# The opening of a decoder block: x by column halves, two weight splits on GpSimd, seven fewer unread products

## The chip, the cores and the metric

The kernel runs on one core of a Trainium2 chip. The metric is the time of one execution on the device in microseconds (us); lower is better. TensorE (PE) multiplies, VectorE (DVE), ScalarE (ACT) and GpSimd (POOL) work element by element, and SyncE (SP) issues nearly all DMAs, in one queue.

## What is computed

One decoder block on 256 tokens of 1024 columns, in float32: a root-mean-square norm of `x`, one combined projection for attention, retention and gates, both branches, a second norm, and a mixture of 32 experts. Around the change only this matters:

```
h = x * lax.rsqrt(jnp.mean(x * x, axis=-1, keepdims=True) + EPS) * g_mix
proj = h @ w_in
```

The later parts (attention, retention, experts, final norm) are the same in both kernels.

## The kernel before

The kernel writes out by hand what each engine does, with a list per engine and semaphores between them. Each engine works through its list strictly in order.

*Float32 products in three parts.* A weight chunk lands in `raw(s)`; ACT rounds it to a high part (`high(Q, s, n)`, one copy of 128x768), and DVE subtracts it from the raw values to a low part (`low(Q, s, n)`). A quad Q has four chunks, s = 0 to 3, and each chunk is used in 18 matmuls of 256 columns in the first two quads. The activation `h`, turned so that columns are on partitions, has a high and a low part too: `normed_high(m)` on ACT and `normed_low(m)` on DVE, m = 0 to 3, two blocks of 128 columns each. PE may start on chunk s of quad 0 when `hT_dve` has reached s + 1 (`normed_low(s)` is done) and `lo_ready` has reached s + 1 (`low(0, s)` is done).

*The opening.* SP issues the two halves of the tokens, t = 0 and 1, as one DMA each (512 KB), then the first weights. For each t ACT squares and sums 1024 columns; DVE scales the sum to a mean square; POOL raises it to the power of minus one half; DVE multiplies the identity by it (`spread`); and PE spreads it over all partitions by a product with ones. ACT copies that to `roots`, and `norm_columns(m)` on DVE multiplies the transposed x by gain and `roots`, two instructions for each m. PE has transposed x in between, into PSUM banks 0 to 3. The first quad writes banks 0 and 1, so that both `norm_columns(0)` and `norm_columns(1)` have to be done before it starts.

*Unread products.* `unread(n)` on PE multiplies the identity by itself n times into a bank that nobody reads. PE runs 6 while x is under way, 2 between the two sets of transposes, 8 behind the product that gives the roots, and 10 more once `norm_columns(0)` is done. The profile counts two records for each of them.

*The order of DVE behind the roots* is written out: `norm_columns(0)`, `norm_columns(1)`, `normed_low(0)`, `low(0,1)`, `normed_low(1)`, and so on. `low(0,0)` stands ahead of the wait for `roots`. SP loads the raw chunk s of quad 1 when `lo_ready` has reached s + 1. POOL has, behind the two powers, four selects of 128x256 that build the attention bias, and then nothing for a long time.

*What follows.* PE goes through four pairs of attention heads, retention, gates and output projection on weights that SP streams in, until the second norm at 322 us. While it does so SP fills free room with the first experts. From 362 us on eight teams of four experts go through PE, each with 24 MB of weights.

Of the kernel before, what the change touches and what calls it, by code (L numbers as in the profile page):

```python
# [24 lines left out]
ALU = mybir.AluOpType  # L25
ACT = mybir.ActivationFunctionType
AX_X = mybir.AxisListType.X
F32 = mybir.dt.float32
# [30 lines left out]
def hybrid_block(nc, x, g_mix, w_in, w_attn, w_ret, w_out, g_ffn, w_router, b_router,  # L59
# [42 lines left out]
    with ExitStack() as ctx:  # L102
# [3 lines left out]
        def sem(name):  # L106
            return ctx.enter_context(nc.semaphore(name))
# [148 lines left out]
        begin_f = gatedT[0:1, PASSES:2 * PASSES]  # L256
        res = hn[:, :, :, :].rearrange("p a k q -> p a (k q)")

        s_x = [sem(f"s_x{t}") for t in range(TT)]
        s_gain = sem("s_gain")  # L260
        s_wr = sem("s_wr")
        s_gk = sem("s_gk")
# [84 lines left out]
        def raw(s, n):  # L347
            return ring[:, 0, s * RAW:s * RAW + n]
# [6 lines left out]
        def is_in_place(Q):  # L355
# [3 lines left out]
        slots = [ring[:, s, :] for s in range(6)] + [oRT_slot[:, :], mid[:, :], store[:, :], hT_slot[:, :],  # L359
                                                         spare[:, :]]  # L360

        MERGED = ((0, 1), (1, 2), (2, 4), (4, 6), (6, 8))
        G_AT, U_AT, D_AT = (3, 4, 5, 10), (7, 0, 1, 2), (8, 9, 6)

# [17 lines left out]
        @block.sync  # L382
        def _(sp):
            for t in range(TT):
                sp.dma_start(xs[:, t, :], x_v[:, t, :]).then_inc(s_x[t], 16)

            def load_quad(Q, piece, after_use=False, fill=(None,) * CH):

# [168 lines left out]
        @block.gpsimd  # L557
        def _(pool):
            link, _n = chain(pool, pool_chain, 0)

            link(pool.memset(ident[:, :], 0.0))
            pool.affine_select(out=ident[:, :], in_=ident[:, :], compare_op=ALU.not_equal, fill=1.0, base=0,
                               pattern=[[-1, P]], channel_multiplier=1).then_inc(const_ready, 1)
            pool.memset(half_neg[:, :], -0.5).then_inc(const_ready, 1)

            def inv_root(n):
                for t in range(TT):
                    pool.wait_ge(ms_done, TT * n + t + 1)
# [12 lines left out]
            pool.affine_select(out=before[:, :], in_=before[:, :], compare_op=ALU.is_gt, fill=0.0, base=0,  # L581
                               pattern=[[1, P]], channel_multiplier=-1).then_inc(const_ready, 1)
            pool.memset(ones[:, :], 1.0).then_inc(const_ready, 1)
            pool.iota(slot_ids[:, :], pattern=[[1, ROUNDS * SLOTS]], base=1, channel_multiplier=0,
                      allow_small_or_imprecise_dtypes=True).then_inc(const_ready, 1)
            pool.iota(rev_ids[:, :], pattern=[[-1, NR]], base=NR, channel_multiplier=0,
                      allow_small_or_imprecise_dtypes=True).then_inc(const_ready, 1)
            pool.iota(expert_ids[:, :], pattern=[[1, E]], base=0, channel_multiplier=0,
                      allow_small_or_imprecise_dtypes=True).then_inc(const_ready, 1)
            link(pool.memset(ident_b[:, :], 0.0))  # L590
            pool.affine_select(out=ident_b[:, :], in_=ident_b[:, :], compare_op=ALU.not_equal, fill=1.0, base=0,
                               pattern=[[-1, NP]], channel_multiplier=1).then_inc(const_ready, 1)
            pool.wait_ge(const_ready, 2)
            inv_root(0)

            for g, (window, _dil) in enumerate(GROUPS):
                if g == 0:
                    pool.wait_ge(dist_done, 1)
                else:
                    pool.wait_ge(dil_done, g)  # L600
                ins = pool.affine_select(out=bias_t[:, g, :], in_=dist if g == 0 else bias_t[:, g, :], compare_op=ALU.is_ge,
                                         fill=MASKED, base=P, pattern=[[-1, T]], channel_multiplier=1)
                if window < T:
                    link(ins)
                    ins = pool.affine_select(out=bias_t[:, g, :], in_=bias_t[:, g, :], compare_op=ALU.is_ge, fill=MASKED,
                                             base=window - P, pattern=[[1, T]], channel_multiplier=-1)
                ins.then_inc(bias_done, 1)
            for i in range(TWOS):
                pool.wait_ge(rvar, i + 1)
                pool.tensor_tensor(out=rstdR[:, :], in0=meanvar[:, :, 1], in1=half_neg[:, :],  # L610
                                   op=ALU.pow).then_inc(rrstd, 1)
            inv_root(1)
            inv_root(2)

        @block.scalar
        def _(act):
            act.dma_start(mix_k[:, :], g_mix.rearrange("(p k) -> p k", k=KT)).then_inc(s_mix, 16)

            def high(Q, s, n):

                act.wait_ge(raw_loaded[s], 32 * Q + 32)
                if not isinstance(Q, int) or Q > 0:

                    act.wait_ge(chunk_used, CH * Q + s + 1 - CH)
                high_of = high_part[:, s, 0:n] if is_in_place(Q) else split[:, s, 0, 0:n]
                act.activation(high_of, raw(s, n), ACT.Copy).then_inc(hi_ready, 1)  # L626

            for t in range(TT):
                act.wait_ge(s_x[t], 16)
                if t > 0:  # L630
                    act.wait_ge(sq_done, t)
                act.activation(junk, xs[:, t, :], ACT.Square, accum_out=ss[:, 0, t:t + 1]).then_inc(sq_done, 1)  # L632

            def normed_high(m):
                act.wait_ge(normed_done, 2 * m + 2)
                act.activation(hT[:, 0, 2 * m:2 * m + 2, :], normed[:, 2 * m:2 * m + 2, :], ACT.Copy).then_inc(hT_act, 1)
# [1 line left out]
            high(0, 0, W_A)  # L638
            act.wait_ge(roots_psum, 1)
            act.activation(roots, bank(4, T), ACT.Copy).then_inc(roots_ev, 1)  # L640
            for m in range(CH):
                normed_high(m)
                if m < CH - 1:
                    high(0, m + 1, W_A)

            def attention(i, n_next):
                for s in range(CH):
# [141 lines left out]
        def _(dve):  # L789
# [22 lines left out]
            for g in range(1, NG):  # L812
# [2 lines left out]
                dve.scalar_tensor_tensor(bias_t[:, g, :], resid_f, MASKED, dist, ALU.mult, ALU.add).then_inc(dil_done, 1)  # L815
                dve.wait_ge(dil_done, g)
            for t in range(TT):
                dve.wait_ge(sq_done, t + 1)
                dve.tensor_scalar(ms[:, 0, t:t + 1], ss[:, 0, t:t + 1], 1.0 / D, EPS, ALU.mult, ALU.add).then_inc(ms_done, 1)
                dve.wait_ge(rstd_done, t + 1)  # L820
                dve.tensor_scalar(spread[:, t, :], ident[:, :], rstd[:, 0, t:t + 1], None, ALU.mult).then_inc(spread_done, 1)
            dve.wait_ge(s_mix, 16)
            low(0, 0, W_A)
            dve.wait_ge(roots_ev, 1)

            def norm_columns(m):

                dve.wait_ge(hT_psum, 3 if m < 2 else 4)
                for k in (2 * m, 2 * m + 1):
                    dve.scalar_tensor_tensor(normed[:, k, :], ps[:, k // 2, (k % 2) * T:(k % 2 + 1) * T], mix_k[:, k:k + 1],  # L830
                                             roots, ALU.mult, ALU.mult).then_inc(normed_done, 1)

            def normed_low(m):
                dve.wait_ge(hT_act, m + 1)
                dve.tensor_tensor(hT[:, 1, 2 * m:2 * m + 2, :], normed[:, 2 * m:2 * m + 2, :],
                                  hT[:, 0, 2 * m:2 * m + 2, :].bitcast(F32), ALU.subtract).then_inc(hT_dve, 1)

            norm_columns(0)
            norm_columns(1)
            normed_low(0)  # L840
            low(0, 1, W_A)
            normed_low(1)
            norm_columns(2)
            low(0, 2, W_A)
            normed_low(2)
            norm_columns(3)
            low(0, 3, W_A)
            normed_low(3)
            dve.wait_ge(bias_done, NG)
# [352 lines left out]
        def _(pe):  # L1202
# [13 lines left out]

            def transpose_rows(t):

                pe.wait_ge(s_x[t], 16)
                rows_t = xs[:, t, :].rearrange("q (p k) -> q k p", k=KT)  # L1220
                for k in range(KT):
                    at = (k % 2) * T + t * P
                    ins = pe.transpose(ps[:, k // 2, at:at + P], rows_t[:, k, :], ident[:, :])
                    if k in (3, 7):
                        ins.then_inc(hT_psum, 1)

# [38 lines left out]
                pe.wait_ge(spread_done, t + 1)  # L1265
                ins = mm(ps[:, 4, t * P:(t + 1) * P], all_ones, spread[:, t, :], True, True)
            ins.then_inc(roots_psum, 1)
            unread(8)
            pe.wait_ge(normed_done, 2)
            unread(10)  # L1270

            with pe.Fori(0, PAIRS) as i:
                queries = columns(NG, 0, W_A)
# [315 lines left out]
```

## Time and profile before

| | before |
|---|---|
| median of 3 runs | 764.15 us (764.02 to 764.28) |
| profiled execution | 763.96 us, its span 762.2 us |
| busy, whole span | PE 599.3 us, DVE 241.5 us, ACT 183.2 us, POOL 11.2 us |
| end of the opening, where the first matmul of quad 0 starts | 12.38 us |

The span begins with the first recorded instruction and ends with the last; 1.8 us of the execution's own time lie outside it. The two times at the ends of the 3 runs are 0.03% apart. All starts below are in us from the start of the span.

### The profile page before, as it was taken

How to read it: one execution, taken by the hardware profiler on the slowest of the kernel's cores; microseconds unless marked ns; L12 is line 12 of the kernel's file. 1: busy time of each engine (PE TensorE's matmuls, PEld its weight loads, DVE VectorE, ACT ScalarE, POOL GpSimd, SP SyncE). 2: the span in 40 equal slices, each digit the busy share in tenths (PEclk: the TensorE clock that was granted, in tenths of full speed). 3: DMA queues.
4: the chain of work that ended last, by engine and by line, in shares of the span. 5: the costliest groups of instructions: out<-in, count | busy, mean ns of one | idle time of the engine just before them, and what ended most of it. 6: DMA issues, size and time to landing. Idle time of an engine off the chain costs nothing.

```text
span 762.2 us, 10787 instructions
## 1 busy us (share of the span) xinstructions
PE 599.3 (79%) x4333; PEld 405.0 (53%) x4333; DVE 241.5 (32%) x411; ACT 183.2 (24%) x250; POOL 11.2 (1%) x31
## 2 busy tenths in 40 slices
PE   9999999999999999999748458458458457556655
PEld 8999999989899999843213113113113113113111
DVE  7667485746554456761010010010010010000001
ACT  5455453644425444341000000000000000000002
POOL 3000000000000000000000000000000000000000
PEclk9999999999999999999979679778877977868979
DMA  8956859564637798979999999999999999999995
GB/s 242 280 158 205 253 151 308 182 202 142 198 119 220 223 329 297 389 312 423 432 426 426 426 427 426 430 426 430 430 423 433 426 423 430 429 426 428 429 416 196
DMA packets 84810, 254.84 MB, mean 334 GB/s; under 512 B 8240, under 2 KB 57392, under 8 KB 72880
## 3 DMA queue, kind: packets, MB, share of 16 engines
q1 hardware_dynamic: 82272, 254.30, 86.6%
q10 hardware_dynamic: 2512, 0.18, 0.2%
q8 instruction: 18, 0.29, 0.1%
q14 instruction: 8, 0.07, 0.0%
HBM read 253.41 MB, written 1.05 MB: 334 GB/s over the span
## 4 chain that ended last, share of the span: by engine, by line
PE 52%; DMA 37%; SPq 7%; ACT 1%; DVE 1%; issue 1%; POOL 0%; POOLq 0%; DVEq 0%; ACTq 0%
PE ps L1204 51%; DMA work<-in_w_down 37%; SPq L540 4%; SPq L492 2%; SPq L461 1%; ACT work L662 1%; DMA store<-in_x 0%; PE ps L1300 0%; PE ps L1410 0%; PE ps L1328 0%; POOL rstd L569 0%; DVE hn L1182 0%; ACT work L632 0%; ACT hn L730 0%; PE ps L1525 0%
## 5 line engine op out<-in xcount | busy, mean ns | idle before, releaser
L1204 PE MATMUL ps<-ring,work 128*32 128x512 f32 x768 | 136.5, 693 | 20.5 <-DMA spare<-in_w_gate 20.3
L1204 PE MATMUL ps<-mid,work 128*32 128x512 f32 (+1 forms) x152 | 77.0, 668 | 71.1 <-DMA ring<-in_w_up 71.1
L1204 PE MATMUL ps<-store,work 128*32 128x512 f32 x128 | 68.3, 692 | 55.5 <-DMA work<-in_w_down 54.1
L1204 PE MATMUL ps<-hT,split 128*128 128x256 f32 x768 | 93.6, 284 | 0.0
L1204 PEld LDWEIGHTS ps<-hT,split 128*128 128x128 f32 x768 | 92.6, 192 | 0.8 <-issue 0.7
L799 DVE TENSOR_TENSOR split<-ring,split 128x768 fp32r<-128x768 f32 (+1 forms) x72 | 73.8, 1045 | 54.8 <-ACT split L626 54.8
L1204 PEld LDWEIGHTS ps<-mid,work 128*32 128x32 f32 (+1 forms) x152 | 20.5, 140 | 125.6 <-DMA ring<-in_w_up 77.5
L1120 DVE TENSOR_TENSOR work<-work,ps 128x512 f32<-128x512 f32 x8 | 5.5, 688 | 240.9 <-PE ps L1204 240.9
L626 ACT ACTIVATE split<-ring 128x768 fp32r<-128x768 f32 (+1 forms) x72 | 64.9, 915 | 70.5 <-PE ps L1204 51.3
L1204 PE MATMUL ps<-split,hT 128*128 128x384 f32 (+1 forms) x384 | 80.4, 365 | 0.0
L1204 PEld LDWEIGHTS ps<-split,hT 128*128 128x128 f32 x384 | 68.8, 188 | 7.8
L1204 PEld LDWEIGHTS ps<-store,work 128*32 128x32 f32 x128 | 15.2, 126 | 101.1 <-DMA work<-in_w_down 57.5
L1204 PE MATMUL ps<-hT_slot,work 128*32 128x512 f32 x128 | 68.3, 692 | 0.0
L1204 PE MATMUL ps<-oRT_slot,work 128*32 128x512 f32 x128 | 68.3, 692 | 0.0
L1204 PEld LDWEIGHTS ps<-ring,work 128*32 128x32 f32 x768 | 33.5, 125 | 65.5 <-issue 40.1
L1204 PE MATMUL ps<-spare,work 128*32 128x512 f32 x128 | 65.0, 665 | 0.0
L796 DVE TENSOR_TENSOR low_part<-ring,high_part 128x1024 fp32r<-128x1024 f32 x36 | 44.1, 1224 | 45.7 <-ACT high_part L626 45.7
L626 ACT ACTIVATE high_part<-ring 128x1024 fp32r<-128x1024 f32 x36 | 38.1, 1058 | 52.7 <-DMA ring<-in_w_in 22.5
L1113 DVE TENSOR_TENSOR work<-ps,gain_s 128x512 f32<-128x512 f32 x14 | 9.7, 692 | 124.1 <-PE ps L1204 124.1
L1204 PE MATMUL ps<-hT,high_part 128*128 128x256 f32 x256 | 46.2, 283 | 0.0
L755 ACT ACTIVATE work<-ps 128x512 f32<-128x512 f32 x8 | 4.8, 597 | 151.0 <-PE ps L1525 151.0
L1204 PE MATMUL ps<-d_home,work 128*32 128x512 f32 x64 | 40.4, 791 | 0.0
(203 smaller groups left out, 779.9 us busy)
## 6 DMA issues: line engine op xcount, KB each, us to landing
ring<-in_w_up SPq DMA_DIRECT2D x21, 2048.0 KB, 43.2
ring<-in_w_gate SPq DMA_DIRECT2D x18, 2048.0 KB, 39.5
ring<-in_w_in SPq DMA_DIRECT2D x80, 256.0 KB, 3.1
ring<-in_w_in SPq DMA_DIRECT2D x96, 192.0 KB, 4.2
mid<-in_w_up SPq DMA_DIRECT2D x7, 2048.0 KB, 34.7
store<-in_w_down SPq DMA_DIRECT2D x6, 2048.0 KB, 34.8
hT_slot<-in_w_down SPq DMA_DIRECT2D x6, 2048.0 KB, 39.2
oRT_slot<-in_w_down SPq DMA_DIRECT2D x6, 2048.0 KB, 43.7
```

Of the source, the lines that this page charges most:

```text
L461: sp.dma_start(slots[at[j]], expert(view, p, j)).then_inc(loaded, 16)
L492: sp.dma_start(d3_home[:, :], expert(wd_v, p, 3)[:, 0:2 * D]).then_inc(down_loaded, 16)
L540: sp.dma_start(to, expert(wd_v, q, j)[:, at:at + n_words]).then_inc(loaded, 16)
L626: act.activation(high_of, raw(s, n), ACT.Copy).then_inc(hi_ready, 1)
L662: act.activation(probsT[u], s_cols(u), ACT.Copy).then_inc(apt_act, 1)
L755: act.activation(hidT.rearrange("p f s -> p (f s)"), bank(0), ACT.Copy).then_inc(hidT_ev, 1)
L796: dve.tensor_tensor(low_part[:, s, 0:n], raw(s, n), high_part[:, s, 0:n].bitcast(F32), ALU.subtract).then_inc(lo_ready, 1)
L799: dve.tensor_tensor(split[:, s, 1, 0:n], raw(s, n), split[:, s, 0, 0:n].bitcast(F32), ALU.subtract).then_inc(lo_ready, 1)
L1113: dve.tensor_tensor(xg[:, steps, :], bank(h).rearrange("p (k s) -> p k s", k=4), gain_s[:, steps].unsqueeze(2).to_broadcast([P, 4, P]), AL ...
L1120: dve.tensor_tensor(hid, sg, bank(3), ALU.mult).then_inc(hid_ready, 1)
L1204: return pe.matmul(o, lhsT=l, rhs=r, start=start, stop=stop, skip_group_check=shared)
```

## The change

Six things are changed, all in the opening.

1. x comes in four DMAs of 256 KB (two column halves of each t) in place of two of 512 KB.
2. ACT squares each half by itself (four squares of 128x512 in place of two of 128x1024). DVE scales the first half's sum ahead of time, and a second instruction of one column adds the other half's.
3. The transposed x goes to PSUM banks 2, 3, 5 and 6, and quad 0 no longer writes over it.
4. DVE does `norm_columns(0)` right behind the roots, then `low(0,0)` and `normed_low(0)`, and only then `norm_columns(1)`.
5. The low parts of chunks 1 and 2 of quad 0 are made by POOL. DVE waits for each at a fixed place in its list (`low_of_pool`), and passes the news on in `lo_ready`.
6. The unread products behind the roots are 6 and 5 in place of 8 and 10.

```diff
-                sp.dma_start(xs[:, t, :], x_v[:, t, :]).then_inc(s_x[t], 16)
+                for h in range(2):
+                    cols = slice(h * HALF, (h + 1) * HALF)
+                    sp.dma_start(xs[:, t, cols], x_v[:, t, cols]).then_inc(s_x[t][h], 16)
...
+            for s in (1, 2):
+                pool.wait_ge(hi_ready, s + 1)
+                pool.tensor_tensor(out=split[:, s, 1, 0:W_A], in0=raw(s, W_A), in1=split[:, s, 0, 0:W_A].bitcast(F32),
+                                   op=ALU.subtract).then_inc(lo_pool, 1)
...
             for t in range(TT):
-                act.wait_ge(s_x[t], 16)
-                if t > 0:
-                    act.wait_ge(sq_done, t)
-                act.activation(junk, xs[:, t, :], ACT.Square, accum_out=ss[:, 0, t:t + 1]).then_inc(sq_done, 1)
+                for h, (part, done) in enumerate(((3, sq_begin), (0, sq_done))):
+                    act.wait_ge(s_x[t][h], 16)
+                    if t > 0:
+                        act.wait_ge(done, t)
+                    cols = slice(h * HALF, (h + 1) * HALF)
+                    act.activation(junk[:, cols], xs[:, t, cols], ACT.Square,
+                                   accum_out=ss[:, part, t:t + 1]).then_inc(done, 1)
...
+                dve.wait_ge(sq_begin, t + 1)
+                dve.tensor_scalar(ms[:, 3, t:t + 1], ss[:, 3, t:t + 1], 1.0 / D, EPS, ALU.mult, ALU.add).then_inc(ms_begin, 1)
+                dve.wait_ge(ms_begin, t + 1)
                 dve.wait_ge(sq_done, t + 1)
-                dve.tensor_scalar(ms[:, 0, t:t + 1], ss[:, 0, t:t + 1], 1.0 / D, EPS, ALU.mult, ALU.add).then_inc(ms_done, 1)
+                dve.scalar_tensor_tensor(ms[:, 0, t:t + 1], ss[:, 0, t:t + 1], 1.0 / D, ms[:, 3, t:t + 1],
+                                         ALU.mult, ALU.add).then_inc(ms_done, 1)
...
+            def low_of_pool(s):
+                dve.wait_ge(lo_pool, s)
+                dve.wait_ge(lo_ready, s)
+                dve.sem_inc(lo_ready, 1)
...
-            unread(8)
+            unread(6)
             pe.wait_ge(normed_done, 2)
-            unread(10)
+            unread(5)
```

The order on DVE in the opening, from the combining of the squares' sums to the end of the opening. In these rows `ms` is written by the scaling, `work<-ident,rstd` is `spread`, `split<-ring,split` is `low`, `hn<-ps,mix_k,work` is `norm_columns` and `hT<-hn,hT` is `normed_low`. Before:

```order
L821 TENSOR_SCALAR work<-ident,rstd 128x128
L799 TENSOR_TENSOR split<-ring,split 128x768
L830 SCALAR_TENSOR_TENSOR hn<-ps,mix_k,work 128x256 x4
L835 TENSOR_TENSOR hT<-hn,hT 128x512
L799 TENSOR_TENSOR split<-ring,split 128x768
L835 TENSOR_TENSOR hT<-hn,hT 128x512
L830 SCALAR_TENSOR_TENSOR hn<-ps,mix_k,work 128x256 x2
L799 TENSOR_TENSOR split<-ring,split 128x768
L835 TENSOR_TENSOR hT<-hn,hT 128x512
L830 SCALAR_TENSOR_TENSOR hn<-ps,mix_k,work 128x256 x2
L799 TENSOR_TENSOR split<-ring,split 128x768
L835 TENSOR_TENSOR hT<-hn,hT 128x512
```

Now:

```order
L840 TENSOR_SCALAR work<-ident,rstd 128x128
L848 SCALAR_TENSOR_TENSOR hn<-ps,mix_k,work 128x256 x2
L814 TENSOR_TENSOR split<-ring,split 128x768
L853 TENSOR_TENSOR hT<-hn,hT 128x512
L848 SCALAR_TENSOR_TENSOR hn<-ps,mix_k,work 128x256 x4
L853 TENSOR_TENSOR hT<-hn,hT 128x512
L848 SCALAR_TENSOR_TENSOR hn<-ps,mix_k,work 128x256 x2
L853 TENSOR_TENSOR hT<-hn,hT 128x512
L814 TENSOR_TENSOR split<-ring,split 128x768
L853 TENSOR_TENSOR hT<-hn,hT 128x512
```

Two of the four `low` rows have left DVE, and the one that stood ahead of the first `norm_columns` stands behind it; the waits for POOL stand between the second and third pair of `norm_columns`, and ahead of the third `normed_low`.

The order on ACT, where `work,ss<-store` is a square, `split<-ring` is `high` and `hT<-hn` is `normed_high`. Before:

```order
L632 ACTIVATE work,ss<-store 128x1024 x2
L626 ACTIVATE split<-ring 128x768
L640 ACTIVATE work<-ps 128x256
L636 ACTIVATE hT<-hn 128x512
L626 ACTIVATE split<-ring 128x768
L636 ACTIVATE hT<-hn 128x512
L626 ACTIVATE split<-ring 128x768
L636 ACTIVATE hT<-hn 128x512
L626 ACTIVATE split<-ring 128x768
L636 ACTIVATE hT<-hn 128x512
```

Now:

```order
L643 ACTIVATE work,ss<-store 128x512 x4
L635 ACTIVATE split<-ring 128x768
L652 ACTIVATE work<-ps 128x256
L648 ACTIVATE hT<-hn 128x512
L635 ACTIVATE split<-ring 128x768 x2
L648 ACTIVATE hT<-hn 128x512 x2
L635 ACTIVATE split<-ring 128x768
L648 ACTIVATE hT<-hn 128x512
```

The high parts of chunks 1 and 2 now stand in one row ahead of the second `normed_high`.

## Rows read from the trace of the kernel before

**Rows 1.** The page: granted clock by 40 slices, and the chain that ended last, by engine.

```profile
PEclk9999999999999999999979679778877977868979
...
PE 52%; DMA 37%; SPq 7%; ACT 1%; DVE 1%; issue 1%; POOL 0%; POOLq 0%; DVEq 0%; ACTq 0%
```

**Rows 2.** Windows (us, then busy us and count by engine, clock, DMA): the stretch after the opening.

```profile
12.38:322.00 309.62, 308.44 (x2292) 291.59 (x2291) 191.24 (x264) 142.80 (x184) 2.03 (x2) 1.00 0.71 226
```

**Rows 3.** The chain of waits, opening: start us, us, what.

```profile
0.78 3.42 DMA store<-in_x
...
8.11 22.83 PE ps L1204 x188
```

**Rows 4.** Timeline of TensorE, opening: start us, us, engine, line, operation, tiles, count.

```profile
8.11 0.49 PE L1204 MATMUL ps<-work 128*128 128x128 f32 x2 [0.34 <-DVE work L821]
8.44 4.18 PE L1204 MATMUL ps<-ident 128*128 128x128 f32 x36
```

**Rows 5.** Timeline of TensorE, the first two quads.

```profile
12.38 17.52 PE L1204 MATMUL ps<-hT,split 128*128 128x256 f32 x144
```

**Rows 6.** Timeline of ScalarE, opening.

```profile
4.22 1.06 ACT L632 ACTIVATE work<-store 128x1024 f32<-128x1024 f32 x1 [1.71 <-DMA store<-in_x]
5.18 0.19 ACT L632 ACTIVATION_READ_ACCUMULATOR work<-store 128x1 f32 x1
5.64 1.06 ACT L632 ACTIVATE work<-store 128x1024 f32<-128x1024 f32 x1 [0.27 <-DMA store<-in_x]
...
9.96 0.63 ACT L636 ACTIVATE hT<-hn 128x512 fp32r<-128x512 f32 x1 [0.95 <-DVE hn L830]
10.50 0.83 ACT L626 ACTIVATE split<-ring 128x768 fp32r<-128x768 f32 x1
```

**Rows 7.** Timeline of VectorE, opening.

```profile
7.65 0.41 DVE L821 TENSOR_SCALAR work<-ident,rstd 128x128 f32<-128x128 f32 x1 [0.67 <-POOL rstd L569]
8.04 0.96 DVE L799 TENSOR_TENSOR split<-ring,split 128x768 fp32r<-128x768 f32 x1
9.05 1.66 DVE L830 SCALAR_TENSOR_TENSOR hn<-ps,mix_k,work 128x256 f32<-128x256 f32 x4
10.63 0.69 DVE L835 TENSOR_TENSOR hT<-hn,hT 128x512 fp32r<-128x512 f32 x1
11.36 0.96 DVE L799 TENSOR_TENSOR split<-ring,split 128x768 fp32r<-128x768 f32 x1
12.24 0.69 DVE L835 TENSOR_TENSOR hT<-hn,hT 128x512 fp32r<-128x512 f32 x1
```

**Rows 8.** Timeline of GpSimd, opening.

```profile
1.21 0.29 POOL L562 TENSOR_SCALAR_AFFINE_SELECT ident<-ident 128x128 f32<-128x128 f32 x1 [0.24 <-POOL ident L561]
...
7.58 0.40 POOL L601 TENSOR_SCALAR_AFFINE_SELECT bias_t<-work 128x256 f32<-128x256 f32 x1
8.12 1.14 POOL L605 TENSOR_SCALAR_AFFINE_SELECT bias_t<-bias_t 128x256 f32<-128x256 f32 x1
9.21 0.74 POOL L601 TENSOR_SCALAR_AFFINE_SELECT bias_t<-bias_t 128x256 f32<-128x256 f32 x2
```

**Rows 9.** Timeline near the end: half squares of the last norm, and their combining.

```profile
754.77 0.60 ACT L766 ACTIVATE work<-ps 128x512 f32<-128x512 f32 x1
...
755.39 0.60 ACT L766 ACTIVATE work<-ps 128x512 f32<-128x512 f32 x1
...
756.18 0.16 DVE L1192 SCALAR_TENSOR_TENSOR ms<-ss,ms 128x1 f32<-128x1 f32 x1
```

**Rows 10.** Windows: DMA while x lands.

```profile
3.00:3.75 0.75, 0.75 (x5) 0.75 (x5) 0.68 (x3) 0.00 (x0) 0.68 (x3) 1.00 1.06 402
```

**Rows 11.** Windows: short and long gaps of TensorE, and the clock behind them.

```profile
350.00:353.00 3.00, 1.41 (x14) 0.92 (x14) 1.02 (x2) 0.60 (x1) 0.00 (x0) 1.00 1.03 431
...
414.00:417.00 3.00, 0.50 (x2) 0.00 (x0) 0.00 (x0) 0.00 (x0) 0.00 (x0) 1.00 1.02 431
417.00:420.00 3.00, 1.97 (x16) 0.64 (x20) 0.00 (x0) 0.00 (x0) 0.00 (x0) 0.86 0.99 421
```

More of the change, by code:

```diff
@@ L257, in hybrid_block @@
         res = hn[:, :, :, :].rearrange("p a k q -> p a (k q)")
-        s_x = [sem(f"s_x{t}") for t in range(TT)]
+        s_x = [[sem(f"s_x{t}{h}") for h in range(2)] for t in range(TT)]
+        sq_begin, ms_begin, lo_pool = sem("sq_begin"), sem("ms_begin"), sem("lo_pool")
         s_gain = sem("s_gain")
@@ L360, in hybrid_block @@
                                                          spare[:, :]]
+        X_BANK = (2, 3, 5, 6)
         MERGED = ((0, 1), (1, 2), (2, 4), (4, 6), (6, 8))
@@ L640, in _ @@
             act.activation(roots, bank(4, T), ACT.Copy).then_inc(roots_ev, 1)
[L641 to L644, printed above, removed]
+            normed_high(0)
+            high(0, 1, W_A)
+            high(0, 2, W_A)
+            normed_high(1)
+            normed_high(2)
+            high(0, 3, W_A)
+            normed_high(3)
             def attention(i, n_next):
@@ L822, in _ @@
             dve.wait_ge(s_mix, 16)
-            low(0, 0, W_A)
             dve.wait_ge(roots_ev, 1)
@@ L829, in norm_columns @@
                 for k in (2 * m, 2 * m + 1):
-                    dve.scalar_tensor_tensor(normed[:, k, :], ps[:, k // 2, (k % 2) * T:(k % 2 + 1) * T], mix_k[:, k:k + 1],
-                                             roots, ALU.mult, ALU.mult).then_inc(normed_done, 1)
+                    dve.scalar_tensor_tensor(normed[:, k, :], ps[:, X_BANK[m], (k % 2) * T:(k % 2 + 1) * T],
+                                             mix_k[:, k:k + 1], roots, ALU.mult, ALU.mult).then_inc(normed_done, 1)
             def normed_low(m):
@@ L836, in normed_low @@
                                   hT[:, 0, 2 * m:2 * m + 2, :].bitcast(F32), ALU.subtract).then_inc(hT_dve, 1)
+            def low_of_pool(s):
+                dve.wait_ge(lo_pool, s)
+                dve.wait_ge(lo_ready, s)
+                dve.sem_inc(lo_ready, 1)
             norm_columns(0)
+            low(0, 0, W_A)
+            normed_low(0)
             norm_columns(1)
-            normed_low(0)
-            low(0, 1, W_A)
+            low_of_pool(1)
+            norm_columns(2)
             normed_low(1)
-            norm_columns(2)
-            low(0, 2, W_A)
+            norm_columns(3)
+            low_of_pool(2)
             normed_low(2)
-            norm_columns(3)
             low(0, 3, W_A)
@@ L1217, in transpose_rows @@
             def transpose_rows(t):
-                pe.wait_ge(s_x[t], 16)
+                for h in range(2):
+                    pe.wait_ge(s_x[t][h], 16)
                 rows_t = xs[:, t, :].rearrange("q (p k) -> q k p", k=KT)
@@ L1222, in transpose_rows @@
                     at = (k % 2) * T + t * P
-                    ins = pe.transpose(ps[:, k // 2, at:at + P], rows_t[:, k, :], ident[:, :])
+                    ins = pe.transpose(ps[:, X_BANK[k // 2], at:at + P], rows_t[:, k, :], ident[:, :])
                     if k in (3, 7):
```

## The prediction, made before the changed kernel ran

> **What bounds the kernel now.** I read the page first. Half of the chain that ended last is PE and over a third DMA; the granted clock is full up to the twentieth slice and uneven behind it, where PE waits for expert weights [rows 1]. So the kernel has two parts: PE sets the pace up to about 362 us, the weight stream from there. Then I asked for windows. From 12.38 to 322 us PE is busy 308.4 of 309.6 us, at full clock [rows 2]. Whatever moves the start of quad 0 and leaves later chunks on time moves all that follows by as much: SP's loads of the experts wait for PE to free their room, so the stream starts earlier or later with PE. I therefore count a microsecond at 12.38 us as a microsecond at the end, and look only for what the opening gains and where it gives it back.
>
> The chain of waits in the opening goes from x's DMA (0.78 to 4.20 us) over squares, power and spread to PE at 8.11, and from there in one piece on PE [rows 3]. That piece deceives: the first 36 records behind the roots' product are unread ones, 4.18 us of them, and they run up to the first product of quad 0 at 12.38 us [rows 4, 5]. DVE had finished `normed_low(0)` at 10.63 + 0.69 = 11.32 us [rows 7]. Two things thus hold the start, and the later is the filler: PE could have begun about 1.0 us earlier. Quad 0 and quad 1 are eight chunks in 17.4 us (12.38 to 29.73, the last part's tail left out), 2.17 us each [rows 5]. Chunk 1 starts at 12.38 + 2.17 = 14.55 us. This is the number to beat.
>
> **x and the squares.** A quarter of x is 256 KB, 0.65 us at 402 GB/s [rows 10]. The order of bytes in the queue is as before, so I let the last quarter land when the second whole did, at 5.62 us (ACT starts on it at 5.64, released by DMA), and the first at 4.20 - 0.65 = 3.55 us [rows 3, 6]. A square of 1024 columns and its sum take 1.16 us (4.22 to 5.37), the half form of the last norm 0.62 from start to start and 0.68 from start to the end of its sum, which is half of the whole's 0.96 and its 0.19 for reading the sum [rows 6, 9]. Four halves from 3.55: 4.22, 4.89, then the last waits for its data and ends at 5.62 + 0.68 = 6.30 us, where the second whole ended at 5.64 + 1.16 = 6.80. The gain is 0.50 us. The bounds: if quarters landed no earlier than wholes, four halves from 4.22 would end at about 6.9, no gain; if the last landed as much as 0.2 us sooner, 0.6 would be the most, since ACT is full. Combining costs one instruction of 0.16 us on the path, in the place of one of 0.15 [rows 9]; its forerunner lies in the time in which DVE waited (0.67 us idle ahead of `spread`) [rows 7]. Two more DMA issues push the first weights' issues back by under 0.9 us. They cost nothing: `low(0,0)` stood ready to run at 8.04 us and is now wanted at 9.4; its cover, if lost, is 1.3 us.
>
> With the same steps behind (power, spread, product, copy), `norm_columns(0)` starts at 9.05 - 0.50 = 8.55 us.
>
> **DVE to chunk 0.** `norm_columns` costs 1.66 / 2 = 0.83 us for one m; `low` 0.88 from start to start (11.36 to 12.24); `normed_low` 0.69 [rows 7]. The new order gives: norm 0 to 9.38, `low(0,0)` to 10.26, `normed_low(0)` to 10.95. `normed_high(0)` starts 0.91 behind the start of the norm, as before (9.05, 9.96), lasts 0.63 and is done by 10.1, hidden behind `low(0,0)` [rows 6]. Taking norm 1 out of the way saves 0.83 us, and putting `low(0,0)` in it costs 0.88: this exchange is worth nothing here. Quad 0 can start at 11.0 us. The unread products permit it: from 7.94 us six of them (0.232 us each, 4.18 / 18 [rows 4]) end at 9.33, five more start at 9.46 and end at 10.6. So the first chunk starts 1.38 us earlier, at 11.0, of which about 0.9 come from the seven unread products that are gone.
>
> **POOL's subtractions and chunk 1.** No row has POOL subtract 768 columns. PE wants chunk 1 at 11.0 + 2.17 = 13.17. ACT now makes the high part of chunk 1 from 9.46 + 0.54 = 10.0 to 10.83 [rows 6], and POOL, whose selects have long ended, may start when DVE ends `normed_low(0)`, at 10.95. Call one subtraction D. DVE does norm 1 to 11.8, then stands at `low_of_pool(1)` until 10.95 + D; queued behind it are norm 2, `normed_low(1)`, for which PE waits, and norm 3. What is late next is therefore DVE's list behind POOL.
>
> The two engines also hold each other up. POOL's select of 256 columns takes 0.40 and 0.37 us, but 1.14 where DVE's `low` ran beside it from 8.04 to 9.00; it ended at 9.26, 0.26 us behind that; it ran undisturbed beside `norm_columns`, which reads PSUM [rows 7, 8]. The other way round, `spread` beside a select (7.58 to 7.98) ended at 8.06, 0.08 us behind it [rows 7, 8]. So I let `normed_low(1)`, wanted at 10.95 + D + 0.05 + 0.83, stand until POOL's second subtraction ends at 10.95 + 2D, and take 0.6 us from there with its start hidden. Chunk 1 then starts at 10.95 + 2D + 0.65 = 11.6 + 2D.
>
> For D the nearest row is the select, one input: 0.29 us for 128 columns and 0.40 for 256 [rows 8], so 0.86 ns a column and 0.18 us fixed. The lower bound is one pass over 768 columns, 0.84 us; the upper one is six whole selects of 0.39 (two inputs, three times the columns), 2.34 us. I take two passes and one fixed part, 0.18 + 2 x 768 x 0.86 ns = 1.50 us, since the subtraction reads two inputs. Chunk 1 then starts at 14.60 us, against 14.55 before: the 1.38 us of the start are all given back. At D = 0.84 nothing is held, chunk 1 starts at 10.95 + 0.84 + 0.05 + 0.83 + 0.69 + 0.05 = 13.41, and 1.14 us are kept. At 2.34 it starts at 16.28, 1.73 late.
>
> The Trainium skill, page "SBUF — State Buffer", section "SBUF: two separate sides", calls the pair of ports that the two engines share an exclusive lock held for the whole instruction. The 1.14 us select agrees; without such a hold on DVE, chunk 1 would start at 10.95 + 1.50 + 1.62 = 14.07. Its "GPSIMD Engine Reference", section 3.1, gives 4497 ns for a two-input float32 operation of 2048 columns and says that VectorE takes half as long. By its share for 768, 1.69 us (an estimate), chunk 1 would start at 14.98 and the kernel be 0.4 us slower; no row of this trace shows such an operation.
>
> **Later chunks.** Behind 14.6 DVE needs norm 3 and `normed_low(2)`, 1.5 us, for a chunk wanted at 16.7, then `low(0,3)` and `normed_low(3)`, 1.6 us, for one wanted at 18.9. Both are in time. The raw loads of quad 1 start later by up to 1.3 us, since `lo_ready` comes later; PE wants that quad's chunks from 19.7 us on at the earliest, five us behind. I cost them at nothing.
>
> **The sum.** -0.50 (squares), 0.0 (exchange on DVE), -0.88 (filler), +1.43 (new wait at chunk 1, 14.60 - 13.17): +0.05 us. Against the profiled execution of 763.96 us (span 762.2 and 1.8 around it, which the change leaves alone) that is 764.0; the median of the runs shown lies 0.19 above it. I predict 764.2 us.
>
> **Rivals.**
> First, POOL is quick, or does not hold DVE. D near 0.84 gives a gain of 1.14 us, 763.0. For it: POOL's selects are as fast as this. Against: they read one input.
> Second, on the other side: POOL is slow. From D = 1.48 on the kernel is slower, and at D = 2.34, six selects, by 1.73 us, 765.9. For it: a select can stretch to 1.14 us when DVE is beside it, and DVE is beside POOL all the time here. Against: behind 10.95 DVE only has `norm_columns` to do until POOL is done, and this did not disturb a select.
> Third, the clock. PE now stands at 10.6 to 11.0 and 13.2 to 14.5. With 1.41 of 3 us busy it kept the full clock; behind 0.50 of 3 us it lost it (0.86 granted in the stretch after) [rows 11]. At the lower level (1.2 GHz) a chunk costs 2.17 us more, 766.4. The new gaps are nearer to the first row.
> Fourth, quarters land late: 0.5 us more on all of the above, 764.7.
>
> **Chances.** A measurement of this kernel can tell about 0.2%, 1.5 us, from no change. The forecast (gain given back at chunk 1, D from 1.1 to 1.9, 763.4 to 765.0) has 0.63; quick POOL 0.20; slow POOL 0.11; clock 0.03; late quarters 0.03. No case but an even larger gain than the start's 1.38 reaches 1.5 us faster: 0.04. Slower by over 1.5 us need D over 2.2 or the clock: 0.10. Within: 0.86. The range is 763.0 to 765.4: it takes in quick POOL and leaves out the far end of slow POOL.
>
> **What would show it.** Second square's sum ends at 6.3; first product of quad 0 at 11.0; POOL's subtraction 1.5 us each; DVE idle behind the second `norm_columns` for 0.6 us and released by POOL; `normed_low(1)` longer than 0.69 us; PE idle ahead of its nineteenth matmul by 1.4 us, released by DVE. Wrong would be: no wait of PE there, a wait at chunk 2 or 3 or in quad 1, or a lower granted clock before 30 us.

## The result, and the profile after

| | before | changed |
|---|---|---|
| median of 7 runs | 764.28 us (764.02 to 764.46) | 767.93 us (765.85 to 769.50) |
| profiled execution (span) | 763.96 us (762.2) | 767.93 us (766.2) |
| first product of quad 0 | 12.38 us | 11.90 us |
| first product of chunk 1 | 14.55 us (worked out) | 16.09 us |
| first product of quad 2 | 29.73 us | 32.79 us |

The medians lie 3.65 us apart, and the ratio on record of the changed kernel to the one before is 1.0037 (95% interval 1.0025 to 1.0050; it is not the quotient of the medians, which is 1.0048): the change makes the kernel slower, by a quarter to half a per cent. I had forecast 764.2 us and no measurable change. The changed kernel's seven runs also scatter over 3.65 us where the seven of the kernel before lie within 0.5. In later sets of 23 to 29 runs, though, the kernel before has single runs up to 769.1 us, so its scatter is not always that small.

The page of the changed kernel shows the same granted clock in its 40 slices as [rows 1], 19 us each, and nearly the same shares in the chain (PE 51% for 52%). At that width next to nothing is to be seen; the difference lies in the first 32 us.

```profile
PEclk9999999999999999999979778877877977868979
...
PE 51%; DMA 37%; SPq 7%; ACT 1%; DVE 1%; issue 1%; POOLq 0%; POOL 0%; DVEq 0%; ACTq 0%
```

ACT in the opening of the changed kernel, to be set beside [rows 6] (start us, us, engine, line, operation, tiles, count, and in brackets the idle time before and who ended it):

```profile
3.51 0.63 ACT L643 ACTIVATE work<-store 128x512 f32<-128x512 f32 x1 [1.00 <-DMA store<-in_x]
4.04 0.19 ACT L643 ACTIVATION_READ_ACCUMULATOR work<-store 128x1 f32 x1
4.35 0.63 ACT L643 ACTIVATE work<-store 128x512 f32<-128x512 f32 x1
4.89 0.19 ACT L643 ACTIVATION_READ_ACCUMULATOR work<-store 128x1 f32 x1
5.30 0.63 ACT L643 ACTIVATE work<-store 128x512 f32<-128x512 f32 x1 [0.22 <-DMA store<-in_x]
5.83 0.19 ACT L643 ACTIVATION_READ_ACCUMULATOR work<-store 128x1 f32 x1
6.29 0.63 ACT L643 ACTIVATE work<-store 128x512 f32<-128x512 f32 x1 [0.27 <-DMA store<-in_x]
6.83 0.19 ACT L643 ACTIVATION_READ_ACCUMULATOR work<-store 128x1 f32 x1
```

The first quarter lands when I had it (3.5 us). The squares of the following ones start 0.8 to 1.0 us apart, not 0.65, and the last square starts at 6.29 us, where that of the second whole started at 5.64. The squares end at 7.02 us, not at 6.30.

DVE and POOL, the same opening, beside [rows 7, 8]:

```profile
9.41 0.88 DVE L848 SCALAR_TENSOR_TENSOR hn<-ps,mix_k,work 128x256 f32<-128x256 f32 x2 [1.07 <-ACT work L652]
10.21 0.95 DVE L814 TENSOR_TENSOR split<-ring,split 128x768 fp32r<-128x768 f32 x1
11.07 0.68 DVE L853 TENSOR_TENSOR hT<-hn,hT 128x512 fp32r<-128x512 f32 x1
11.68 0.87 DVE L848 SCALAR_TENSOR_TENSOR hn<-ps,mix_k,work 128x256 f32<-128x256 f32 x2
13.80 0.88 DVE L848 SCALAR_TENSOR_TENSOR hn<-ps,mix_k,work 128x256 f32<-128x256 f32 x2 [1.26 <-DVEq L859]
14.60 1.35 DVE L853 TENSOR_TENSOR hT<-hn,hT 128x512 fp32r<-128x512 f32 x1
```

```profile
11.77 3.63 POOL L615 TENSOR_TENSOR split<-ring,split 128x768 fp32r<-128x768 f32 x2 [2.25 <-ACT split L635]
```

DVE's order, a wait of DVE for POOL there, and a stretched `normed_low(1)` (1.35 us in place of 0.68) are as predicted: POOL's second subtraction ends at 11.77 + 3.63 = 15.40, and the stretched instruction 0.55 us behind. But a subtraction takes 1.82 us, not 1.50, and the wait is 1.26 us, not 0.6.

PE, beside [rows 5]: chunk 0, then a gap of 1.78 us (1.4 predicted), then seven chunks. The windows under it show the clock (us, busy us and count of PE, PEld, DVE, ACT and POOL, granted clock, DMA share, GB/s).

```profile
11.90 2.41 PE L1228 MATMUL ps<-hT,split 128*128 128x256 f32 x18 [0.17 <-DVE hT L853]
16.09 16.87 PE L1228 MATMUL ps<-hT,split 128*128 128x256 f32 x126 [1.78 <-DVE hT L853]
```

```profile
14.00:16.00 2.00, 0.31 (x3) 0.11 (x1) 2.00 (x4) 1.28 (x2) 1.40 (x1) 1.00 0.58 163
17.00:20.00 3.00, 3.00 (x16) 3.00 (x16) 2.67 (x4) 1.41 (x3) 0.00 (x0) 0.50 0.56 154
20.00:22.00 2.00, 2.00 (x18) 2.00 (x18) 0.96 (x1) 0.57 (x1) 0.00 (x0) 0.93 0.55 126
```

Behind the gap the clock is granted at 0.50 of full speed (1.2 of 2.4 GHz): 16 matmuls in 3 us, where the kernel before does the 18 of a chunk in 2.17. Seven chunks need 16.70 us (16.09 to 32.79) where they needed 15.18 (14.55 to 29.73). So the opening is 1.54 us late at chunk 1 and 3.06 us at quad 2. At the end of the span the two profiled executions are 4.0 us apart.

### The profile page after: what moved, and what is told of

It reads as the page before. It is cut to its first block, busy times and chain, and to the rows that moved or that the text cites. A ratio compares the mean times of both kernels' runs of the same rounds, so it can differ in the third digit from the quotient of the medians.

```text
span 766.2 us, 10773 instructions
## 1 busy us (share of the span) xinstructions
PE 600.3 (78%) x4319; PEld 405.4 (53%) x4319; DVE 240.7 (31%) x411; ACT 184.1 (24%) x254; POOL 14.1 (2%) x33
## 4 chain that ended last, share of the span: by engine, by line
PE 51%; DMA 37%; SPq 7%; ACT 1%; DVE 1%; issue 1%; POOLq 0%; POOL 0%; DVEq 0%; ACTq 0%
PE ps L1228 50%; DMA work<-in_w_down 37%; SPq L544 4%; SPq L496 2%; SPq L465 1%; ACT work L677 1%; PE ps L1325 0%; PE ps L1435 0%; PE ps L1353 0%; DVE hn L1206 0%; DVE hT L853 0%; ACT hn L745 0%; DVE hn L848 0%; PE ps L1550 0%; DVE work L1144 0%
## 5 line engine op out<-in xcount | busy, mean ns | idle before, releaser
L1228 PE MATMUL ps<-hT,split 128*128 128x256 f32 x768 | 95.4, 286 | 1.9 <-DVE hT L853 1.9
L814 DVE TENSOR_TENSOR split<-ring,split 128x768 fp32r<-128x768 f32 (+1 forms) x70 | 72.0, 1047 | 55.4 <-ACT split L635 55.4
```

Of the source, the lines that this page charges most:

```text
L814: dve.tensor_tensor(split[:, s, 1, 0:n], raw(s, n), split[:, s, 0, 0:n].bitcast(F32), ALU.subtract).then_inc(lo_ready, 1)
L1228: return pe.matmul(o, lhsT=l, rhs=r, start=start, stop=stop, skip_group_check=shared)
```

## The experiments

All shifts below are against the kernel before. "Quad 2" is how much later than 29.73 us the first product of quad 2 starts in the profile, in us; "output" is the time of the stage of gates and output weights, from its first chained product to the norm's transposes, 90.90 us before; "median" is the difference of the medians of runs on the same chip (5 to 12 of each kernel, 7 to 29 of the one before); the ratio has its 95% interval.

| kernel | unread behind the roots | quad 2 | output, us | median | ratio |
|---|---|---|---|---|---|
| changed | 11 | +3.06 | 91.02 | +3.65 | 1.0037 (1.0025, 1.0050) |
| d1 whole x | 11 | +2.68 | 90.90 | +3.16 | 1.0038 (1.0024, 1.0052) |
| a1 gap filled | 20 | +1.72 | 92.57 | +3.73 | 1.0041 (1.0025, 1.0056) |
| l1 changed, 18 unread | 18 | +2.16 | 90.91 | +3.39 | 1.0052 (1.0037, 1.0067) |
| c1 splits on DVE | 11 | +0.53 | 92.12 | +1.62 | 1.0019 (1.0010, 1.0028) |
| h1 order and unread alone | 11 | +0.14 | 92.28 | +1.30 | 1.0013 (1.0004, 1.0022) |
| m1 the same, 28 nops | 11 | +0.09 | 92.35 | +0.97 | 1.0014 (1.0006, 1.0023) |
| b1 11 unread alone | 11 | -0.93 | 91.28 | +0.21 | 1.0001 (0.9991, 1.0012) |
| j1 the same, 28 nops | 11 | -0.94 | 92.28 | +0.06 | 0.9999 (0.9991, 1.0008) |
| k1 8 and 3 wide | 11 | -0.09 | 92.25 | +0.80 | 1.0006 (0.9995, 1.0017) |
| g1 halves alone | 18 | +0.40 | 90.90 | +0.87 | 1.0019 (1.0008, 1.0031) |
| f1 POOL's splits alone | 18 | +1.41 | 90.91 | +1.38 | 1.0020 (1.0011, 1.0029) |
| p1 the same, narrow | 18 | +2.84 | 90.89 | +2.25 | 1.0023 (1.0013, 1.0034) |
| e1 later start | 27 | +1.92 | 90.92 | +1.90 | 1.0028 (1.0017, 1.0039) |
| n1 narrow | 18 | -0.17 | 90.91 | -0.68 | 0.9985 (0.9977, 0.9994) |

**First set: the clock, the filler, the splits, the halves.**

```diff
# a1, from the changed kernel
-            unread(5)
+            unread(14)
# b1, from the kernel before
-            unread(8)
+            unread(6)
-            unread(10)
+            unread(5)
# c1, from the changed kernel (POOL's loop goes)
-            low_of_pool(1)
+            low(0, 1, W_A)
-            low_of_pool(2)
+            low(0, 2, W_A)
# d1, from the changed kernel: x in two DMAs, two squares, one scaling, as before
```

a1: 

> The changed kernel with 14 in place of 5 unread products behind norm_columns(0), so that PE works until about 13.6 us and starts quad 0 there, 1.7 us later than the changed kernel. Theory C (clock): chunk 1 still starts at 16.1 us (POOL and DVE decide), but without a gap ahead of it the granted clock stays at 1.00; the 1.6 us lost between chunk 1 and the end of quad 1 are gone: about 766.0 us, and the runs lie within 0.5 us of each other as those of the kernel before do. Rival S (supply: only the lateness of the chunks counts): a later chunk 0 gains nothing, 767.9 us, and the runs scatter over 3 us as before.

PE of a1, and the granted clock behind it:

```profile
13.65 2.39 PE L1228 MATMUL ps<-hT,split 128*128 128x256 f32 x18
16.24 15.37 PE L1228 MATMUL ps<-hT,split 128*128 128x256 f32 x126 [0.20 <-DVE hT L853]
```

```profile
16.00:18.00 2.00, 1.80 (x15) 1.77 (x15) 2.00 (x5) 1.28 (x3) 0.00 (x0) 1.00 0.68 179
18.00:20.00 2.00, 2.00 (x19) 2.00 (x18) 2.00 (x4) 1.14 (x2) 0.00 (x0) 1.00 0.48 134
```

Theory C held up to quad 2: the clock stayed full, and though chunk 0 starts 1.75 us later than in the changed kernel, quad 2 starts 1.34 us earlier. The forecast of the end failed: the median is 768.1 us and the runs scatter over 2.8 us (766.0, 767.5, 767.6 and three at 768.7), close to what rival S had said. In the profiled execution, one of the slowest, the gain was lost again at 293 to 303 us, where PE waits 1.5 us for output weights, which it does not in the changed kernel's profile. So a1 shows what the gap does to the clock, and no gain in time.

b1: 

> The kernel before with 6 and 5 unread products behind the roots in place of 8 and 10, nothing else. normed_low(0) is done at 11.3 us, and the low parts of chunks 1 to 3 come at 12.9, 15.2 and 17.4 us, ahead of a PE that would want them at 13.6, 15.7 and 17.9. Theory: PE starts at 11.4 us, never waits behind that, and the kernel gains 1.0 us: 763.3 us. Rival: with its filler gone PE idles a little ahead of quad 0 and the granted clock falls: 765 us or more, scattered.

Quad 0 starts at 11.44 us and nothing waits, as expected; the clock holds. But the 0.93 us are gone at the end: 764.60 us, no change. Neither theory had this.

c1: 

> The changed kernel with the low parts of chunks 1 and 2 on DVE again, at the two places at which it waits for POOL. Theory (POOL's two subtractions of 1.8 us are what makes chunk 1 late): DVE needs 0.9 us for the low part and nothing holds it, chunk 1 starts at about 14.9 us, a gap of 0.8 us on PE leaves the clock alone: 764.6 to 764.9 us with little scatter. Rival (the later landing of x and the order are what costs): still 767 us or more.

Chunk 1 starts at 14.96 us behind a gap of 0.62 us at full clock, against 16.09. By the shifts the kernel gains 2.0 us on the changed one by taking the two subtractions from POOL. Its median, 766.0 us, misses both forecasts all the same: it is 1.1 us slower than its opening explains, as b1.

d1: 

> The changed kernel with x in two DMAs and two squares as before; order, POOL's splits and the unread products stay changed. Theory (halves cost because they land later: the last square ended at 7.02 us against 6.80): the roots come 0.36 us earlier, at 9.05 us, chunk 1 at 15.7 us, its gap on PE stays at 1.8 us and so the clock still falls: 767.5 us, scattered over 2 us or more. Rival (the halves cost nothing): 767.9 us. Should it be under 766 us, the halves would be the main cause.

Chunk 1 at 15.72 us behind a gap of 1.79 us, the clock falls to 0.50 again, and the median is 767.55 us: as expected by the first theory, but for the scatter, which is 0.8 us and not 2.

**Second set: each part alone.**

```diff
# e1, from the kernel before
-            unread(10)
+            unread(19)
# f1, from the kernel before: POOL's loop of the changed kernel, and on DVE
-            low(0, 1, W_A)
+            low_of_pool(1)
-            low(0, 2, W_A)
+            low_of_pool(2)
# g1, from the kernel before: the changed kernel's four DMAs, four squares and combining
# h1, from d1: as c1, both low parts on DVE
```

e1: 

> The kernel before with 19 in place of 10 unread products behind norm_columns(0): quad 0 starts 9 x 0.232 = 2.1 us later, at 14.5 us, PE has no gap and all chunks are ready. It measures what a microsecond at the start of quad 0 is worth at the end. One for one (my prediction's assumption): 766.4 us. Theory T (the weight stream is near its limit from about 270 us on and adds to a delay): 766.9 to 768 us, with a wait of PE for the output weights around 290 us in the trace. If a start that comes later costs less than 1.5 us, the stream hides part of it.

One for one: quad 0 starts at 14.30 us, 1.92 late, and the median is 1.90 late. No wait at the output weights.

f1: 

> The kernel before with only the low parts of chunks 1 and 2 on POOL (order of the norms, x, banks and unread products as before). By 1.82 us for a subtraction: the first ends at about 13.2 us, the second holds normed_low(1) until 15.0, chunk 1 starts at 15.6 us against 14.55, a gap of 1.0 us on PE without a fall of the granted clock, so 1.05 us late at 31 us, and 765.3 us one for one, 766 us if the stream adds its part. If POOL's subtractions were harmless: 764.4 us.

DVE and PE of f1:

```profile
13.53 2.16 DVE L841 TENSOR_TENSOR hT<-hn,hT 128x512 fp32r<-128x512 f32 x1 [2.11 <-DVEq L847]
```

```profile
12.34 2.40 PE L1215 MATMUL ps<-hT,split 128*128 128x256 f32 x18
15.83 15.48 PE L1215 MATMUL ps<-hT,split 128*128 128x256 f32 x126 [1.09 <-DVE hT L841]
```

`normed_low(1)` follows the wait at once here and is held for 2.16 us, until 0.56 us behind POOL's second subtraction (11.51 + 3.62 = 15.13). It is the hold of the changed kernel at twice the length. The gap is 1.09 us, the clock stays full, and the cost passes through one for one (+1.41 at quad 2, +1.38 in the median).

g1: 

> The kernel before with only the column halves (four DMAs of x, four squares). The roots come 0.36 us later, as in the changed kernel, and with them the 18 unread products and quad 0: 764.7 us, one for one. If halves gained what I had predicted (0.5 us), 763.8 us, and if they cost nothing 764.4.

The last square starts at 6.34 us, against 5.64 of the second whole. Halves cost 0.40 us at quad 2, as this run's forecast had it, where the prediction had a gain of 0.50. The median is 0.87 us up; no trace shows where the other 0.47 went.

h1: 

> The changed kernel with x whole and both splits on DVE: what stays is the new order of the norms and splits, the banks and the 11 unread products. Quad 0 starts at 11.45 us; DVE then has norm, low part, norm and normed_low(1) ahead of chunk 1, 3.1 us, which is ready at 14.5 us: a gap of 0.9 us on PE, and nothing gained or lost against 14.55: 764.3 us. If the order itself were harmful: 765.5 us or more; if its early start were kept: 763.4.

The opening is as expected, with chunk 1 at 14.57 us behind a gap of 0.63. The end is 1.3 us late, and three of its eleven runs lie at 764.0 to 764.4, the others at 765.1 to 766.8.

PE of b1, and of h1 behind chunk 0:

```profile
11.44 17.53 PE L1204 MATMUL ps<-hT,split 128*128 128x256 f32 x144
```

```profile
14.57 15.46 PE L1214 MATMUL ps<-hT,split 128*128 128x256 f32 x126 [0.63 <-DVE hT L839]
```

h1 and b1 differ in the new order and the banks alone. They start quad 0 within 0.1 us of each other (11.54 and 11.44), but b1 goes on without a gap, and at quad 2 h1 is 1.07 us behind it: in the new order `low(0,0)` and `norm_columns(2)` stand between the roots and `normed_low(1)`, DVE reaches that 1.5 us later than in b1 (13.75 for 12.21), and the 0.9 us that fewer unread products give are gone. The new order (or the banks with it) thus costs a microsecond of its own, without POOL.

**Third set: the microsecond behind the opening.** Up to here the four kernels other than d1 and the changed one that have 11 or 20 unread products lose 0.4 to 1.7 us in the output stage, and none of those with 18 or 27. The profile shows one queue that fetches instructions by DMA in 18 blocks of 16 KB. Their places move when only PE's list gets shorter, so I take them for PE's. In the kernel before one is fetched at 286.4 us, and in the kernels with 11 products 3 to 6 us later in the program (the 5 to 6 us are those of kernels that have waited in this stage by then), beside other weights.

```diff
# j1, from b1, and m1, from h1
+            for _i in range(14):
+                pe.nop(nofuse=True)
             pe.wait_ge(const_ready, 1)
...
+            for _i in range(14):
+                pe.nop(nofuse=True)
             pe.wait_ge(normed_done, 2)
# k1, from the kernel before
-            unread(10)
+            for _i in range(3):
+                mm(ps[:, 7, 0:427], ident[:, :], xs[:, 0, 0:427], True, True)
# l1, from the changed kernel: unread(8) and unread(10) as before
```

j1: 

> The kernel with 11 unread products (its quad 0 starts 0.94 us earlier than in the kernel before) plus 28 empty instructions on PE's list, 14 at its start and 14 ahead of the wait for norm_columns(0), where PE's list waits anyway: as many instructions as the 7 missing products took. So PE's list is as long as before and its blocks are fetched at the same places of the program. Theory F (the shift of PE's instruction fetches, which take one of the 16 DMA engines each, delays weights in the stages where the stream is near its limit): no extra 1.1 us, the early start is kept, 763.5 us. Rival R (the extra microsecond is chance or follows the start time): 764.6 us as with 11 alone.

m1: 

> The new order alone with 11 unread products (chunk 1 at 14.6 us, as before), plus the same 28 empty instructions on PE. Theory F: the 1.3 us that this kernel lost behind its opening are gone: 764.5 us with little scatter. Rival R: 765.7 us as without them.

By the times rival R is met in both. As tests of theory F they are inconclusive: the 28 empty instructions did not move the fetches. They stand at the same places of the program as in k1, to 0.8 us or better up to the stage's 50th microsecond, and the extra microsecond stays.

k1: 

> The kernel before with its last 10 unread products of 128 columns replaced by 3 of 427, about the same time on PE with 28 instructions less in its list; quad 0 starts at 12.4 us give or take 0.3. Theory F: the fetches come where they come with 11 unread products, and the kernel is slower by about 1.1 us though its opening is unchanged: 765.5 us, scattered over 2 us. Rival R: 764.4 us, within 0.4 us.

The chain of waits of k1 in the output stage (start us, us, what), and that of the kernel before:

```profile
231.13 46.09 PE ps L1204 x384
...
277.24 5.76 DMA ring<-in_w_ret
...
292.13 4.57 DMA ring<-in_w_out
```

```profile
231.21 90.90 PE ps L1204 x672
```

With an opening 0.09 us early the kernel is 0.80 us later in the median, and its fastest run (764.74) is slower than 17 of the 29 of the kernel before. Its loads of `w_ret` land in 5.3 us in the median of 268 to 292 us, where the kernel before has 3.7; DVE and ACT get their chunk late, and PE waits twice. Theory F's forecast is met in place and in size (0.9 against 1.1), though the interval of the ratio reaches to no change. How the fetches would do it is not shown: while the late load is under way, from 277.24 to 283.00 us, no instruction block is fetched (the nearest ones of this queue are at 274.67 and 292.32).

l1: 

> The changed kernel with 8 and 10 unread products as before. Quad 0 starts at 12.8 us, chunk 1 still at 16.1 to 16.2, the gap on PE shrinks from 1.8 to 1.2 us, at which another kernel kept its clock: so 1.7 us late at 30 us, without the 1.5 us of the clock. By theory F the list is as long as before and nothing is added behind: 766.1 us. If the clock were not what costs: 767.9 us.

In the profile (766.5 us, the fastest of its runs) the gap is 1.03 us, the clock holds, and the output stage takes 90.91 us. Its third quarter of x landed late (squared from 6.15), so that chunk 1 starts at 16.67. The median is 768.0 us with runs up to 771.3: the forecast of 766.1 failed, and 767.9, where I had put it if the clock were not what costs, is met. What the slower runs did is not known; they may have lost the clock, but no trace shows it.

**Fourth set: the gap alone, and the length alone.**

```diff
# n1, from the kernel before, and p1, from f1
-            unread(8)
+            narrow(8)
             pe.wait_ge(normed_done, 2)
-            unread(10)
+            narrow(10)
# narrow(n): n times mm(ps[0:64, 7, 0:64], ident[:, 0:64], ident[:, 0:64], True, True)
```

n1: 

> The kernel before with its 18 unread products behind the roots made of 64 x 64 in place of 128 x 128 words: as many instructions, half the time each, so quad 0 starts at 11.4 us as with 11 products (0.9 us early) and PE's list keeps its length. Theory F (the length of PE's list decides where its instruction blocks are fetched, and with the short list the weights of the output stages come late): the gain is kept, 763.5 us. Rival R (the extra microsecond comes with an early start or by chance): 764.4 us or more.

763.75 us against 764.43, ratio 0.9985 (0.9977 to 0.9994): the only kernel faster than the one before. It has an early start with the length of list of the kernel before. Its profile is of its slowest run and doesn't show that start: x landed 0.7 us late there, and quad 0 starts at 12.20 us. In p1, with the same filler and x on time, it starts at 11.62, 0.76 us early, so that a median 0.68 us better is nearly the whole of it. PE's chain in the output stage is whole again:

```profile
231.03 90.91 PE ps L1204 x672
```

This execution is 0.17 us early there and 1.0 late at the end of the span (763.2 for 762.2): it lost more than a microsecond among the experts, which nothing here explains.

p1: 

> The kernel before with POOL's two subtractions (chunk 1 starts at 15.8 us, 765.8 us in its earlier run with a gap of 1.1 us on PE) and the same 64 x 64 unread products: chunk 0 starts 0.9 us earlier, chunk 1 still at 15.8, so the gap grows to 2.0 us. Theory C (the granted clock falls behind a gap near 2 us): the clock is 0.5 for some 3 us behind chunk 1, PE ends quad 1 at 32.6 in place of 31.1 us, and the kernel is slower by 1.5 us than with the gap of 1.1: 767.3 us, though nothing but an earlier chunk 0 has changed. Rival (the clock holds at 2 us): 765.8 us.

PE of p1, and its clock:

```profile
11.62 2.40 PE L1215 MATMUL ps<-hT,split 128*128 128x256 f32 x18
15.88 16.86 PE L1215 MATMUL ps<-hT,split 128*128 128x256 f32 x126 [1.86 <-DVE hT L841]
```

```profile
16.00:18.00 2.00, 2.00 (x11) 2.00 (x12) 1.30 (x4) 1.36 (x2) 0.00 (x0) 0.53 0.76 220
18.00:20.00 2.00, 2.00 (x13) 2.00 (x13) 2.00 (x4) 1.27 (x2) 0.00 (x0) 0.61 0.08 18
```

Chunk 1 starts as in f1 (15.88 and 15.83 us), chunk 0 0.72 us earlier, the gap is 1.86 us, and the seven chunks take 16.69 us to quad 2 in place of 15.31. This is the clock's price by itself: 1.38 us in the profiles. The runs form two groups: five at 765.4 to 765.7, where f1's runs are, and seven at 766.6 to 768.1. The median is 0.92 us over f1's, the upper group's about 1.4. That the lower group kept its clock is my reading of their times; only one execution has a trace. It would explain the scatter of the changed kernel too, but d1, which lost the clock in its profile, scatters over 0.8 us alone.

## Why the prediction was wrong

**Right.** That chunk 1 is the place, that DVE waits for POOL there and is then held by POOL's second subtraction. With the measured start of POOL (11.77) and D = 1.82, the working's last step gives 11.77 + 3.64 + 0.65 = 16.06 us; it was 16.09. The start of quad 0 came as early as the later roots allowed (11.90, 0.90 behind my 11.0). The exchange on DVE was worth nothing at quad 0 (11.54 us in h1, 11.44 in b1); what it costs at chunk 1 I did not look at by itself, and there h1 starts at 14.57 us where b1's chunk 1, worked out, is at 13.6. And a microsecond at quad 0 was one at the end in e1 and f1.

**The squares, -0.50 predicted.** This step failed by 0.86 us: `norm_columns(0)` starts at 9.41, not 8.55. 0.72 of it stand at the end of the squares (7.02 for 6.30), 0.14 in the steps between them and the norm. I let the last quarter land when the second whole had, from the argument that the order of bytes in the queue is the same. It landed about 0.65 us later, and ACT, which then still had a whole half to square, could not make it good. My own bound (no gain if quarters landed like wholes) was too kind: I gave late quarters a chance of 0.03 and a price of 0.5 us. g1, with the halves alone, shows the sign: +0.40 at quad 2.

**POOL's D, 1.50 us predicted.** 1.82 measured, 0.32 more, twice over: 0.64. The value lay inside my bounds, and the estimate from the Trainium skill's "GPSIMD Engine Reference", section 3.1, 1.69, was nearer. Both mis-sized terms make 1.50 us, all of the 1.49 by which chunk 1 missed its 14.60. By themselves they move the forecast from 764.2 to 765.7 us, already past the 765.4 at which the range ended.

**The clock, chance 0.03.** This step doubled the miss: 1.52 us more at quad 2. I weighed a gap of 1.4 us against one row with 1.41 of 3 us busy that kept the clock and one with 0.50 of 3 that lost it [rows 11], and took the near one. It was not as near as it looked. PE in that stretch of the kernel before:

```profile
351.36 0.75 PE L1525 MATMUL ps<-ident,work 128*128 128x128 f32 x4 [0.90 <-DVE work L1120]
352.79 0.62 PE L1204 MATMUL ps<-store,work 128*32 128x512 f32 x1 [0.69 <-ACT work L755]
```

The idle time is two gaps of 0.90 and 0.69 us with work between them, and no row that I had shows one gap of 1.4. The gap was 1.78 us. In the profiles of these openings the clock held behind gaps of 0.62, 0.63, 1.03 and 1.09 us and fell behind 1.78, 1.79 and 1.86; 1.4 itself was in none. The rivals were not independent: the slow POOL or late quarters widen the very gap that the clock depends on, so their prices add. I had priced each against the forecast alone, and a sum of three small misses was in no case.

**What was in no part of it.** This is 4.0 - 3.06, the 0.9 us between quad 2 and the end of the span (0.6 by the medians). Part of it is the first stream of down weights, which takes 37.68 us in the changed kernel and 36.63 before, but it takes 37.5 in f1 and 36.5 in p1 too, and I cannot tie it to a cause. The removal of seven products also shortens PE's list. b1 and n1 differ in this and in how the filler is made: +0.21 and -0.68 us. That the shorter list costs up to 1 us is suggested by k1 and n1 together and not shown, since k1's interval reaches to no change and those of b1 and n1 touch; that the moved fetches do it is argued from their places, and in k1 none falls into the late load. Against it stand the changed kernel and d1, which have the short list and in their profiles a whole output stage, and a1, whose list is 8 instructions longer than before and whose stage is the longest. It stays open.

## What to carry to other kernels

Filler that keeps PE busy should end where the work after it can go on without a gap: starting chunk 0 earlier while chunk 1 stays late made this kernel slower (p1 against f1), and starting it 1.75 us later gave 1.34 us back at quad 2 (a1), though not in the median. Before counting on an early first chunk, work out the start of the second with the same care: the new order left the first where it was and made the second 1 us later (h1 against b1). Where several small delays feed one wait, add their prices before judging whether the clock holds. A second engine that is half as fast and holds the first one up is no help on the way to the next chunk. And time a removal of instructions against a form with the same length of list before calling the gain or loss its own.

## What was not expected of the hardware

- Two subtractions of 128x768 on POOL took 3.62 to 3.64 us in every profile that has them, 1.9 times DVE's 0.95 each, and held a DVE subtraction of two SBUF inputs for up to 2.16 us in place of 0.68.
- Four DMAs of 256 KB in place of two of 512: the last square started at 6.29, 6.32, 6.34, 6.45 and 6.86 us in five kernels, against 5.51 to 5.64 (and in one run 6.38) with two.
- The granted clock fell to 0.50 for about 3 us behind one gap of 1.8 us on PE. In the changed kernel PE had been at work from 8.40 us to 14.31 ahead of it, but for 0.17.
- One stage, which begins some 220 us behind the opening, was 0.4 to 1.7 us longer in seven of the nine kernels with 11 or 20 unread products and in none of the six with 18 or 27 (k1's 8 and 3 counted as 11), though the kernels differ in the opening alone. Why is open.
